# Sums of three RMS norms as products with a full tile of ones, root and reciprocal taken in the accumulator

## What is computed

```python
def rmsnorm(x, g):
    y = x * lax.rsqrt(jnp.mean(x * x, axis=-1, keepdims=True) + EPS)
    return y * g

def head_rmsnorm(y, g, n_heads):
    yh = y.reshape(b, s, n_heads, w // n_heads)
    yh = yh * lax.rsqrt(jnp.mean(yh * yh, axis=-1, keepdims=True) + EPS)
    return yh.reshape(b, s, w) * g

# first block
y = concatenate([head_rmsnorm(y_a, gn_a, 8), head_rmsnorm(y_b, gn_b, 8)]) @ w_out   # head norm
x = x + g1 * y
h = modulate(rmsnorm(x, norm2_g), sh2, sc2)                                          # second norm
x = x + g2 * peer(h, w_q, sub_keys, expert_u, expert_v)
# second block
...
return rmsnorm(h, norm_final_g)                                                      # last norm
```

## Time and profile before

| | |
|---|---|
| median of 3 runs | 2212.12 us (2211.29 to 2212.75) |
| profiled execution, its own time | 2212.41 us |
| its span | 2211.1 us |
| TensorE, matmul | 2143.4 us busy, 97% |
| VectorE | 1615.6 us busy, 73% |
| ScalarE | 1001.1 us busy, 45% |
| GpSimd | 964.9 us busy, 44% |
| mean granted TensorE clock | 0.986 |

### The profile page before, as it was taken

How to read it: one execution, slowest core, us unless ns; L and a number is a source line. 1 busy time by engine, 2 the same in 40 slices (tenths; PEclk the granted TensorE clock), 3 DMA queues, 4 the chain that set the end, 5 groups by cost and what they waited for, 6 DMA issues and landing times.

```text
span 2211.1 us, 30449 instructions
## 1 busy us (share of the span) xinstructions
PE 2143.4 (97%) x11336; PEld 1944.8 (88%) x11336; DVE 1615.6 (73%) x2793; ACT 1001.1 (45%) x1814; POOL 964.9 (44%) x635
## 2 busy tenths in 40 slices
PE   6999999999999999999999999999999899999998
PEld 3777899999999999999999999988877788888887
DVE  6784579998987998999999999848565474443323
ACT  4433443578787773333333333534454443232222
POOL 0435336778654335665767766433323321111000
PEclk9999999999999999999999999999999999999999
DMA  8646236787879999999999999624242432333332
GB/s 311 197 137 228 96 101 170 199 214 184 227 226 343 339 342 366 390 410 410 411 407 411 409 411 403 196 82 139 72 122 69 167 107 94 98 95 96 102 94 81
DMA packets 195802, 494.95 MB, mean 224 GB/s; under 512 B 33084, under 2 KB 84412, under 8 KB 194944
## 3 DMA queue, kind: packets, MB, share of 16 engines
q1 hardware_dynamic: 131720, 311.51, 41.7%
q0 software_dynamic: 63936, 181.50, 23.3%
HBM read 433.31 MB, written 57.28 MB: 222 GB/s over the span
## 4 chain that ended last, share of the span: by engine, by line
PE 55%; DVE 15%; DMA 10%; issue 3%; ACT 2%; POOL 1%; DVEq 0%; SPq 0%; ACTq 0%
PE bank L579 10%; PE bank L580 10%; PE bank L583 10%; DMA scores<-in_rows_v,row_at 6%; PE bank_pair L583 4%; PE bank_pair L579 4%; PE bank_pair L580 4%; DVE scores L2101 4%; DMA scores<-in_rows_u,row_at 3%; DVE scores L2095 3%; DVE weights_lo L1678 3%; DVE hidden L2146 2%; PE bank_stat L956 1%; PE bank_pair L827 1%; PE bank_stat L957 1%
## 5 line engine op out<-in xcount | busy, mean ns | idle before, releaser
L1140 ACT ACTIVATE weights_hi<-weights_raw 128x1024 fp32r<-128x1024 f32 (+1 forms) x411 | 431.8, 1051 | 320.9 <-DMA weights_raw<-in_expert_v 205.6
L579 PE MATMUL bank<-h_lo,weights_hi 128*128 128x384 f32 (+1 forms) x1484 | 521.0, 351 | 8.1 <-DVE gates L2363 3.8
L580 PE MATMUL bank<-h_hi,weights_hi 128*128 128x384 f32 (+1 forms) x1484 | 518.3, 349 | 0.0
L1678 DVE TENSOR_TENSOR weights_lo<-weights_raw,weights_hi 128x1024 fp32r<-128x1024 f32 x347 | 438.4, 1264 | 68.5 <-ACT weights_hi L1140 66.7
L583 PE MATMUL bank<-h_hi,weights_lo 128*128 128x384 f32 (+1 forms) x1484 | 306.5, 347 | 0.7 <-DVE weights_lo L1678 0.7
L579 PEld LDWEIGHTS bank<-h_lo,weights_hi 128*128 128x128 f32 x1484 | 281.6, 190 | 23.1 <-DVE gates L2363 3.9
L580 PEld LDWEIGHTS bank<-h_hi,weights_hi 128*128 128x128 f32 x1484 | 281.4, 190 | 13.6
L583 PEld LDWEIGHTS bank<-h_hi,weights_lo 128*128 128x128 f32 x1484 | 264.1, 188 | 14.1 <-DVE weights_lo L1678 1.0
L2538 POOL DMA_INDIRECT scores<-in_rows_u,row_at x128 | 179.1, 1399 | 208.1 <-DVE row_coef L2095 180.6
L2551 POOL DMA_INDIRECT expert_coefs<-square x128 | 227.4, 1777 | 96.3 <-issue 48.8
L2488 POOL TENSOR_TENSOR weights_lo<-weights_raw,weights_hi 128x1024 fp32r<-128x1024 f32 x64 | 157.7, 2469 | 239.7 <-ACT weights_hi L1140 239.4
(11 more groups left out here) (599 smaller groups left out, 4013.9 us busy)
## 6 DMA issues: line engine op xcount, KB each, us to landing
weights_raw<-in_expert_u SPq DMA_DIRECT2D x128, 512.0 KB, 4.5
weights_raw<-in_expert_v SPq DMA_DIRECT2D x128, 512.0 KB, 7.1
weight<-expert_coefs POOLq DMA_DIRECT2D x32, 768.0 KB, 10.0
hidden_store<-hidden SPq DMA_DIRECT2D x28, 768.0 KB, 5.8
hidden<-hidden_store POOLq DMA_DIRECT2D x28, 768.0 KB, 13.3
expert_coefs<-stage SPq DMA_DIRECT2D x16, 1024.0 KB, 8.1
ada_raw<-in_w_ada SPq DMA_DIRECT2D x26, 512.0 KB, 6.4
weights_raw<-in_w_ffn_gate SPq DMA_DIRECT2D x22, 512.0 KB, 3.5
```

Source lines behind the costliest of these rows:

```text
L579: M.matmul(bank[:, 0:width], hi[:, c:c + P], m_lo[k][:, 0:width], start=start and i == 0, stop=False)
L580: M.matmul(bank[:, 0:width], hi[:, c:c + P], m_hi[k][:, 0:width], start=False, stop=False)
L1140: S.activation(w_hi[n % SPLIT][:, 0:w], w_raw[n % RAW][:, 0:w], ACT.Copy).then_inc(*hi_done.inc(n))
L1678: V.tensor_tensor(w_lo[n % SPLIT][:, 0:w], w_raw[n % RAW][:, 0:w], w_hi[n % SPLIT][:, 0:w].bitcast(F32), ALU.subtract).then_inc(*lo_dve.in ...
```

## The change

The sums of the head norm become one product per tile: a stationary tile `head_ones` (128x128, two blocks of 64x64 ones, else zeros, f32, written by GpSimd at the start) by the whole square of 128x512, into a bank of its own from `take`. The bank then holds in every channel its head's sum. ScalarE takes the root of the bank in place, VectorE the reciprocal in place, and then multiplies y by gain and bank as before. Expansions, spreads and small reciprocals go. The orders are rewritten: sums 4 and 5 stand before product 17, sums 6 and 7 after it, 0 and 1 before product 19 and 2 after it, and 3 after the w_out products with tiles 4 to 7; on ScalarE the roots stand between squares and highs. In the second and the last norm, two products of the full `ones` with 256 columns take the place of the 8 one-column matmuls; root and reciprocal are taken in the bank's half, and the spread goes.

```diff
-        expanded = [a_square, sb("expanded", [P, T], F32, scope)]
+        head_ones = sb("head_ones", [P, P], F32, scope)
...
             def head_sums(tiles):
                 for c in tiles:
+                    bank = take(("head_sum", c))
                     M.wait_ge(*act["head_square", c])
-                    sums(("head_sum", c), [square[:, c % 2, :]], HEAD_SUMS + 8 * c, groups=True)
-            def head_spreads(tiles):
...
-            M.wait_ge(*act["x_root"])
-            head_sums([4, 5, 6, 7])
+                    M.matmul(bank[:], head_ones[:], square[:, c % 2, :], start=True, stop=True).then_inc(*pe.inc(("head_sum", c)))
+
+            M.wait_ge(*pool["head_ones", 1])
+            head_sums([4, 5])
             product(("in", 17), 17, h_hi_tiles, h_lo_tiles)
-            head_spreads([4, 5, 6, 7])
+            head_sums([6, 7])
             product(("in", 18), 18, h_hi_tiles, h_lo_tiles)
-            M.wait_ge(*act["head_root", 4])
-            head_sums([0, 1, 2])
+            head_sums([0, 1])
             product(("in", 19), 19, h_hi_tiles, h_lo_tiles)
+            head_sums([2])
...
-            head_spreads([0, 1, 2])
             out_tiles([4, 5, 6, 7])
-            M.wait_ge(*act["head_root", 0])
             head_sums([3])
             out_tiles([0, 1, 2])
-            head_spreads([3])
             out_tiles([3])
...
             def half_sums(name, t):
+                bank = take((name + "_sum", t))
                 M.wait_ge(*act[name + "_square", KD - 1, t])
-                sums((name + "_sum", t), [scaled[:, 0, :], square[:, 1, :]], 0, blocks=(2 * t, 2 * t + 1))
+                M.matmul(bank[:, HALVES[t]], const("ones"), scaled[:, 0, HALVES[t]], start=True, stop=False)
+                M.matmul(bank[:, HALVES[t]], const("ones"), square[:, 1, HALVES[t]], start=False, stop=True) \
+                    .then_inc(*pe.inc((name + "_sum", t)))
...
-            spread(("x1_spread", 0), 0, blocks=(0, 1))
...
-                        spread(("x1_spread", 1), 0, blocks=(2, 3))
...
-            spread(("x4_spread", 0), 0, blocks=(0, 1))
...
-            spread(("x4_spread", 1), 0, blocks=(2, 3))
...
             def root_half(name, t):
                 S.wait_ge(*pe[name + "_sum", t])
-                root((name + "_root", t), 2 * t, 2, D)
+                at = banks[name + "_sum", t][:, HALVES[t]]
+                S.activation(at, at, ACT.Sqrt, bias=col("eps"), scale=1.0 / D).then_inc(*act.inc((name + "_root", t)))
...
+            def head_roots(tiles):
                 for c in tiles:
+                    S.wait_ge(*pe["head_sum", c])
+                    S.activation(banks["head_sum", c][:], banks["head_sum", c][:], ACT.Sqrt, bias=col("eps"), scale=1.0 / HEAD_DIM) \
+                        .then_inc(*act.inc(("head_root", c)))
...
-            head_squares([4, 5, 6, 7])
+            head_squares([4, 5])
+            head_roots([4, 5])
+            head_squares([6, 7])
             gate_copy(3)
-            head_expand([4, 5, 6, 7])
-            head_hi([4, 5, 6, 7])
+            head_hi([4, 5])
+            head_roots([6, 7])
+            head_hi([6, 7])
             split_hi(18 + 3)
-            head_squares([0, 1, 2])
+            head_squares([0, 1])
+            head_roots([0, 1])
             split_hi(19 + 3)
-            head_expand([0, 1, 2])
-            head_hi([0, 1, 2])
+            head_squares([2])
+            head_hi([0, 1])
+            head_roots([2])
+            head_hi([2])
             head_squares([3])
-            head_expand([3])
+            head_roots([3])
             head_hi([3])
...
             def head_norms(tiles):
                 for c in tiles:
-                    V.wait_ge(*pe["head_spread", c])
+                    V.wait_ge(*act["head_root", c])
+                    chain(V.reciprocal(banks["head_sum", c][:], banks["head_sum", c][:]))
...
-            head_rstd([4, 5, 6, 7])
             ada_tile(27)
             ada_tile(28)
             head_norms([4, 5, 6, 7])
             conv_mult(3)
             ada_tile(29)
             ada_tile(30)
-            head_rstd([0, 1, 2])
             conv_gate(3)
             ada_tile(31)
             ada_tile(32)
             head_norms([0, 1, 2])
-            head_rstd([3])
             head_norms([3])
...
             def h2_scaled(t, k):
                 if k == 0:
-                    V.wait_ge(*pe["x1_spread", t])
+                    V.wait_ge(*act["x1_root", t])
+                    chain(V.reciprocal(banks["x1_sum", t][:, HALVES[t]], banks["x1_sum", t][:, HALVES[t]]))
...
                 add_half("x4", "down", t)
-                rstd(("x4_root", t), ("x4_rstd", t), 2 * t, 2)
-                V.wait_ge(*pe["x4_spread", t])
+                V.wait_ge(*act["x4_root", t])
+                chain(V.reciprocal(banks["x4_sum", t][:, HALVES[t]], banks["x4_sum", t][:, HALVES[t]]))
...
             G.memset(zeros[:], 0.0).then_inc(*pool.inc("zeros"))
+            G.memset(head_ones[:], 0.0).then_inc(*pool.inc("head_zeros"))
+            G.wait_ge(*pool["head_zeros"])
+            for h in range(2):
+                r = slice(h * HEAD_DIM, (h + 1) * HEAD_DIM)
+                G.memset(head_ones[r, r], 1.0).then_inc(*pool.inc(("head_ones", h)))
+                G.wait_ge(*pool["head_ones", h])
```

More of the change, by code:

```diff
@@ L780, in tensor @@
                             block_over[n] = ("q", h)
-                    if t == 0 and k == 1:
-                        M.wait_ge(*dve["x1_rstd", 1])
-                        spread(("x1_spread", 1), 0, blocks=(2, 3))
             for h in range(HEADS + 1):
@@ L1111, in tensor @@
             down_high(1, 0)
-            M.wait_ge(*act["x3_root"])
             M.wait_ge(*pool["x4_added", 6])
@@ L1243, in head_squares @@
                     S.activation(square[:, c % 2, :], y[:, c, :], ACT.Square).then_inc(*act.inc(("head_square", c)))
-                at = HEAD_SUMS + 8 * tiles[0]
-                S.wait_ge(*pe["head_sum", tiles[-1]])
-                root(("head_root", tiles[0]), at, 8 * len(tiles), HEAD_DIM)
-            def head_expand(tiles):
+            def head_roots(tiles):
                 for c in tiles:
-                    at = HEAD_SUMS + 8 * c
-                    if c == tiles[0]:
-                        S.wait_ge(*dve["head_rstd", c])
-                    if c in (6, 7):
-                        S.wait_ge(*pe["head_spread", c - 2])
-                    if c in (0, 1):
-                        S.wait_ge(*pe["head_spread", 6 + c])
-                    if c in (2, 3):
-                        S.wait_ge(*pe["head_spread", c - 2])
-                    S.activation(expanded[c % 2][:].rearrange("p (n d) -> p n d", d=HEAD_DIM),
-                                 rms[:, at:at + 8].unsqueeze(2).broadcast_to([P, 8, HEAD_DIM]), ACT.Copy) \
-                        .then_inc(*act.inc(("expanded", c)))
+                    S.wait_ge(*pe["head_sum", c])
+                    S.activation(banks["head_sum", c][:], banks["head_sum", c][:], ACT.Sqrt, bias=col("eps"), scale=1.0 / HEAD_DIM) \
+                        .then_inc(*act.inc(("head_root", c)))
             def head_hi(tiles):
@@ L1848, in vector @@
             ada_tile(26)
-            def head_rstd(tiles):
-                rstd(("head_root", tiles[0]), ("head_rstd", tiles[0]), HEAD_SUMS + 8 * tiles[0], 8 * len(tiles))
             def head_lo(c):
@@ L1868, in head_norms @@
                         V.wait_ge(*pool["y_lo", 5])
-                    if c in (2, 3):
-                        V.wait_ge(*pe["head_sum", 2 if c == 2 else 3])
-                    V.scalar_tensor_tensor(temporary(c), y[:, c, :], col("gn", c), banks["head_spread", c][:], ALU.mult, ALU.mult) \
-                        .then_inc(*dve.inc(("head_spread", c)))
-                    dve.also(("y_scaled", c), ("head_spread", c))
+                    V.scalar_tensor_tensor(temporary(c), y[:, c, :], col("gn", c), banks["head_sum", c][:], ALU.mult, ALU.mult) \
+                        .then_inc(*dve.inc(("head_sum", c)))
+                    dve.also(("y_scaled", c), ("head_sum", c))
                     if c != tiles[0]:
@@ L1920, in vector @@
             split_lo(BLOCK_AT["w_q", 1] + 1)
-            rstd(("x1_root", 0), ("x1_rstd", 0), 0, 2)
             add_half("x1", "out", 1, ada[:, 23:24])
@@ L1943, in vector @@
                         h2_lo(t, k - 1)
-                    if t == 0 and k == 1:
-                        rstd(("x1_root", 1), ("x1_rstd", 1), 2, 2)
                 h2_lo(t, KD - 1)
@@ L2469, in vector @@
                 add_half("x4", "down", t)
-                rstd(("x4_root", t), ("x4_rstd", t), 2 * t, 2)
-                V.wait_ge(*pe["x4_spread", t])
+                V.wait_ge(*act["x4_root", t])
+                chain(V.reciprocal(banks["x4_sum", t][:, HALVES[t]], banks["x4_sum", t][:, HALVES[t]]))
                 for k in range(KD):
                     V.scalar_tensor_tensor(x[:, k, HALVES[t]], x[:, k, HALVES[t]], col("norm_final", k),
```

(2 more changed lines are left out.)

15 lines of the change are left out of this document (2 added, 13 removed).

## The result

The changed kernel takes 2236.3 us (median of 4 runs, 2234.36 to 2237.28) where the kernel before takes 2211.7 us (median of 4, 2210.67 to 2212.75): the ratio is 1.0104, its 95% interval 1.0092 to 1.0117. It is slower by 1%. The forecast was 2235.6 us.

The account below looks back on a forecast made before the run. TensorE, busy 97% of the span, was taken as the bound, with the head norm becoming VectorE's; 20.8 + 2.1 + 0.6 = 23.5 us more gave 2235.9 us against the profiled execution, 2235.6 for the median, range 2227 to 2243.

Parts of the forecast that it names:

- The price: VectorE's reciprocal in the accumulator goes by elements in a partition: 3.34 us for 512, 1.75 us for 256.
- the Trainium skill's repeat count: Rival reading: 8 cycles an element, 4.3 us a 512-wide reciprocal, 8.6 us over the forecast; chance 0.03.
- First group: Head norm, tiles 4 to 7: VectorE's reciprocals make GpSimd start the low of tile 7 10.4 us later.
- What moves along: Work queued behind tile 7's low (weight lows, adaLN loads, product 19, gate product, tile 0's norm) shifts by the same 10.4 us.
- Second group: Head norm, tiles 0 to 3: tile 0's norm to TensorE's last products takes 23.8 us, before 13.2; +10.6 us.
- Head stage: Both groups of the head norm together, until TensorE's last products there: +20.8 us.
- Second norm: Half-width reciprocals of 1.75 us enter VectorE's chain; TensorE's 0.8 us backlog absorbs the first part: +2.1 us.
- Last norm: End of kernel: first half's reciprocal hidden, final chain 3.3 us instead of 2.3, less 0.4 saved on TensorE: +0.6 us.
- An ordinary pass: Rival: the accumulator reciprocal takes 0.69 us for 512, so not slower than before, 2209 to 2211 us; chance 0.04.
- Slower by less: Rival: head delay cut mid-stage if adaLN loads land sooner and the clock doesn't fall while idle; 2228 us, chance 0.15.
- Slower by more: Rival: TensorE's lower clock persists, second norm lacks backlog, reciprocals exceed 3.34 us; up to 2244 us, chance 0.12.

Follow-up runs that it names:

- e1: The changed kernel without the eight 512-wide VectorE reciprocals of the head norm, y scaled by the root itself; 2210.92 us, ratio 0.9994.
- e5: The changed kernel with unread filler products on TensorE in its two long head-stage waits, 84 before sum 0 and 70 before sum 3; 2237.13 us, ratio 1.0106.
- e8: The kernel before with only product 17 moved between head sums 5 and 6; 2212.47 us, ratio 0.9994.
- e4: The changed kernel with root and reciprocal in one ScalarE pass (Abs_reciprocal_sqrt) in all three norms, no VectorE reciprocal there; 2206.35 us, ratio 0.9974.
- e7: The one-pass reciprocal-root kernel with product 19 before sums 0 and 1, and GpSimd's weight low 19 before y lows 5 and 7; 2202.12 us, ratio 0.9949.

## Why the prediction was right

The time, 2236.3 us against 2235.6 forecast, came out in the main by the steps named, with two misses of 0.9 us that cancel. Relative to before, less the 1.8 us with which this execution began late:

- **The price.** 3.34 us forecast, 3.36 measured; 1.75 and 1.76 for 256. Eight rows in SBUF and 128 rows in the accumulator cost the same, so the slope in elements of a partition was the right reading. 4.3 us, as the estimate by the Trainium skill's repeat count had it, it is not. (By the prediction's own 0.95 us for each 0.1 us, that rival would have been 9.1 us over the forecast, not 8.6.)
- **First group, +10.4.** GpSimd starts the low of tile 7 at 176.84, 12.2 later than before, less 1.8: 10.4.
- **What moves along.** The adaLN tile after the wait was put at about 186, and starts at 188.29 - 1.8 = 186.5; the gate product at 188.8, and it is at 190.84 - 1.8 = 189.0. Product 19 was to end at 188.0, its first 5 us at the lower level. It ends at 186.2 by this count (188.0 in the trace), since its matmuls are back at full pace from 182.8, 1.6 us after its start. That changed nothing, as the loads came later. The norm of tile 0 starts at 196.53 - 1.8 = 194.7 where 194.1 was forecast: +10.9 instead of +10.3.
- **Second group.** From there to TensorE's last products 24.0 us against 23.8. The largest single difference is sum 3 with its hand-over, 2.1 us (211.45 to 213.54) for 1.9. The wait before sum 3 is 17.1 us where 12 was named: TensorE was done with tiles 4 to 7 at 194.4, earlier than I took it to be, and sum 3 waits for VectorE either way.
- **Head stage.** +21.7 for +20.8, the +0.9 in the two lines above.
- **Second norm, the term mis-sized for this execution.** From the add at 257.97 to the first scaled tile it is 1.26 us longer, 1.25 forecast. But the stage is 1.2 us longer, not 2.1. I took the lengths from one execution of the kernel before, and its TensorE had a granted clock of 0.79 in that place. The add of the second half, 8.3 us behind the split at 227.29 there, comes 7.2 us behind the same split in after. From the add to VectorE's last low it is 2.9 us longer, as forecast. So the steps on VectorE held, and what was wrong was to take the add, and the 0.8 us that TensorE was behind, as fixed. It isn't the delayed head that shortens the stretch: e1, whose head stage is not late, has the same 78.5 us.
- **Last norm, +0.6.** From the start of the sums to the first result it is 3.42 us for 3.3 forecast (before 2.32), and with the 0.4 that TensorE saves ahead of it the end gives 0.6. The rows of the chain that ended last, after, beside the earlier trace rows:

```profile
2224.17 0.67 PE bank_pair L741 x2
2224.84 0.45 PE bank_pair L742 x2
...
2225.31 0.46 ACT bank_pair L1139
...
2225.79 1.78 DVE bank_pair L2440
...
2227.59 3.22 DVE residual L2442 x8
```

**The rivals.** "An ordinary pass" is refuted by the rows of the reciprocals; e1 shows what it would have given, about no change, as forecast for it (2209 to 2211). "Slower by less" had two conditions, and e5 meets the one on the clock: with it at 1.00 the stage is 1.9 us shorter and the time is not, since the loads decide there with product 19. "Slower by more" had three; the reciprocal is over by 0.02 us, not 0.1, TensorE's lower level didn't outlast tile 3, and the second norm came out shorter than forecast, not longer. That a delay of the head passes on in full stands in the table: 23.5 us at its end, 24.7 behind the second norm, 21.3 ahead of the last products, in a middle stretch that moves by 3 us from one execution to the next. The agreement to 0.7 us is luck in part: the head stage was 0.9 us over its term and the second norm 0.9 under, and single executions of the kernel before lay between 2208.1 and 2219.5 us in the course of the study.

Where my expectations failed most was in gains. For e1 and e8 I summed a chain's savings and did not ask, as the prediction did for losses, what is late next. Both times it was TensorE's own work in front of or behind sum 3, part of it at the lower level.

## What to carry to other kernels

Spreading a statistic to all channels by a product with ones saves TensorE time, but every elementwise operation after it then runs over the full width: price each by elements in a partition, and look on which engine's chain it lands. A VectorE reciprocal at 6.2 ns an element is the one to keep on the small tensor, or, where its accuracy is enough, to replace by a function that ScalarE evaluates within the root's own pass (e4). And once a chain is shorter, look for what is late next before booking the gain: here it was a load behind another engine's subtraction, and moving that, with a product, brought e7 a further quarter of a per cent.

## What the runs showed of the hardware

- A VectorE reciprocal costs the same with source and result in the accumulator on 128 partitions (3.36 us for 512) as in SBUF on 8 (3.34 us), and 1.76 us for 256: (3361 - 1759) / 256 = 6.26 ns an element, with next to no fixed cost (1.76 x 2 - 3.36 = 0.16 us, what the smallest take).
- ScalarE's reciprocal root takes the time of its root, 654 ns for 128x512 in the accumulator, with a table load of 1.28 us when the function changes.
- Two convolution passes of VectorE, each with two tensor sources in SBUF, take 1.54 us in the kernel before, at 170.94, and took 5.50 us in after, at 178.43. GpSimd subtracted two weight blocks in that very time:

```profile
178.07 5.31 POOL L2457 TENSOR_TENSOR weights_lo<-weights_raw,weights_hi 128x1024 fp32r<-128x1024 f32 x2
```

Before, GpSimd had ended its two at 170.62, just ahead of VectorE's, after 4.70 us. The Trainium skill (SBUF — State Buffer, SBUF: two separate sides) says that such a pass of VectorE and an operation of GpSimd lock each other out of a shared pair of ports for the length of an instruction. The rows agree with taking turns: GpSimd 2.4 us, VectorE 0.7, GpSimd 2.4, VectorE 0.7 from 178.07 on would have GpSimd done at 183.6 and VectorE at 184.3, where the rows have 183.38 and 183.93. It was not tried by itself. VectorE then waited 4.35 us for a load all the same.
